# Projections of the mixer branches as three products of rounded high and low parts

## What is computed

```python
def trunk_layer(x, cond, P, l, ctx):
    ...
    ob = chunk_gmlp(bu, bv, P['b_v_norm'][l], P['b_ws'][l], P['b_bs'][l])
    ...
    gates = jax.nn.sigmoid(gl.astype(jnp.float32)).astype(x.dtype).reshape(b, s, N_BRANCH, D_MODEL)
    merged = (gates[:, :, 0] * (oa.reshape(b, s, A_Q) @ P['w_a_o'][l])
              + gates[:, :, 1] * (ob @ P['w_b_o'][l])
              + gates[:, :, 2] * (oc.reshape(b, s, C_Q) @ P['w_c_o'][l]))
    x = x + g1 * (merged @ P['w_out'][l])
    ...
    x = x + g2 * expert_choice_moe(h2, P['w_router'][l], P['b_router'][l], P['w_gate'][l], P['w_up'][l], P['w_down'][l])
    return x, new
```

## Time and profile before

| | us |
|---|---|
| median of 3 runs | 2548.26 (2548.24 to 2552.01) |
| profiled execution | 2548.74 |
| its span, first to last instruction | 2546.9 |
| TensorE busy (matmul) | 2301.7, 90% |
| weight loads | 1765.2, 69% |
| VectorE busy | 1641.2, 64% |
| ScalarE busy | 1205.8, 47% |
| GpSimd busy | 283.7, 11% |

### The profile page before, as it was taken

How to read it: one execution, slowest core, us unless ns; L and a number is a source line. 1 busy time by engine, 2 the same in 40 slices (tenths; PEclk the granted TensorE clock), 3 DMA queues, 4 the chain that set the end, 5 groups by cost and what they waited for, 6 DMA issues and landing times.

```text
span 2546.9 us, 37561 instructions
## 1 busy us (share of the span) xinstructions
PE 2301.7 (90%) x14585; PEld 1765.2 (69%) x14585; DVE 1641.2 (64%) x1927; ACT 1205.8 (47%) x1348; POOL 283.7 (11%) x246
## 2 busy tenths in 40 slices
PE   3998899999769999999959988999995999999997
PEld 1777779899546666666647777898994666666664
DVE  1345545534768889888942465454355888988885
ACT  3223323312257777777732232233122677777773
POOL 1012000001121111110011020000012101111101
PEclk8999999999879999999969999999996999999998
DMA  9351110105589999999944410111154999999995
GB/s 333 133 172 63 53 59 34 59 34 182 206 301 365 374 373 373 373 379 375 366 148 166 168 67 20 59 34 59 53 198 167 337 372 373 373 374 376 378 377 184
DMA packets 271390, 566.10 MB, mean 222 GB/s; under 512 B 10568, under 2 KB 12680, under 8 KB 271216
## 3 DMA queue, kind: packets, MB, share of 16 engines
q1 hardware_dynamic: 254848, 509.64, 55.5%
q0 software_dynamic: 14512, 48.05, 6.4%
q10 hardware_dynamic: 1904, 6.62, 0.7%
HBM read 542.71 MB, written 24.18 MB: 223 GB/s over the span
## 4 chain that ended last, share of the span: by engine, by line
PE 83%; DVE 5%; DMA 4%; issue 4%; ACT 3%; DVEq 0%; POOL 0%; SPq 0%; ACTq 0%; POOLq 0%
PE ps L1069 39%; PE ps L770 26%; PE ps L918 6%; PE ps L852 3%; PE ps L894 2%; DMA ring<-in_w_down 2%; PE ps L877 1%; PE ps L710 1%; PE ps L724 1%; DMA ring<-in_w_mod 1%; PE ps L1059 1%; PE ps L988 1%; DVE w_lo L1794 1%; DMA ring<-in_w_in 1%; ACT w_hi L1378 1%
## 5 line engine op out<-in xcount | busy, mean ns | idle before, releaser
L1794 DVE TENSOR_TENSOR w_lo<-ring,w_hi 128x2048 fp32r<-128x2048 f32 x378 | 864.6, 2288 | 134.9 <-ACT w_hi L1378 134.1
L1378 ACT ACTIVATE w_hi<-ring 128x2048 fp32r<-128x2048 f32 x384 | 736.7, 1920 | 315.8 <-PE ps L1069 257.8
L1069 PE MATMUL ps<-w_hi,xT 128*80 128x512 f32 x2048 | 649.1, 396 | 2.2 <-DVE xT L1800 2.2
L770 PE MATMUL ps<-WH,HTH 128*128 128x256 f32 x1840 | 540.3, 294 | 14.7 <-ACT Y L1304 9.0
L770 PE MATMUL ps<-ringL,HTH 128*128 128x256 f32 x1840 | 520.1, 283 | 0.0
L770 PE MATMUL ps<-WH,HTL 128*128 128x256 f32 x1840 | 519.6, 282 | 0.0
L1069 PEld LDWEIGHTS ps<-w_hi,xT 128*80 128x80 f32 x2048 | 306.0, 149 | 173.1 <-issue 4.6
L1069 PE MATMUL ps<-w_lo,xT 128*80 128x512 f32 x1024 | 406.0, 397 | 0.0
L770 PEld LDWEIGHTS ps<-WH,HTH 128*128 128x128 f32 x1840 | 351.6, 191 | 42.2 <-issue 23.1
L770 PEld LDWEIGHTS ps<-ringL,HTH 128*128 128x128 f32 x1840 | 351.9, 191 | 0.8
L770 PEld LDWEIGHTS ps<-WH,HTL 128*128 128x128 f32 x1840 | 351.0, 191 | 0.0
(11 more groups left out here) (198 smaller groups left out, 2145.0 us busy)
## 6 DMA issues: line engine op xcount, KB each, us to landing
ring<-in_w_gate SPq DMA_DIRECT2D x128, 1024.0 KB, 11.3
ring<-in_w_up SPq DMA_DIRECT2D x128, 1024.0 KB, 10.2
ring<-in_w_down SPq DMA_DIRECT2D x128, 1024.0 KB, 11.8
ring<-in_w_mod SPq DMA_DIRECT2D x23, 2048.0 KB, 8.1
ring<-in_w_in SPq DMA_DIRECT2D x18, 2048.0 KB, 7.9
ring<-in_w_out SPq DMA_DIRECT2D x4, 2048.0 KB, 10.6
ring<-in_w_o SPq DMA_DIRECT2D x4, 1536.0 KB, 6.4
Y<-x_save POOLq DMA_DIRECT2D x10, 512.0 KB, 7.4
```

The costliest lines, as they stand in the source:

```text
L770: last = nc.tensor.matmul(dst, a[:, t, k], w, start=k == 0 and i == 0, stop=k == KB - 1 and i == 2)
L1069: last = nc.tensor.matmul(ps[0:CE, bank], lhs[:, a, kb], w[:, u, k], start=kb == 0 and i == 0, stop=kb == KB - 1 and i == 2)
L1378: nc.scalar.activation(w_hi[:, u % UB], ring[:, raw[0], 4 * (u % 2):4 * (u % 2) + 4], ACT.Copy).then_inc(hi_ready, 1)
L1794: TT(w_lo[:, u % UB], ring[:, raw[0], 4 * (u % 2):4 * (u % 2) + 4], w_hi[:, u % UB].bitcast(f32), ALU.subtract).then_inc(lo_ready, 1)
```

## The change

Both operands of a projection are split into high and low parts and the projection becomes three f32r products for each 128 rows of w_o. New tiles of the type f32r lie over existing ones (`QKr` over `QK`, `Yr` over `Y`, `SCr` over `SC`), in regions that are free at the time.

```diff
+        qoH = QKr[:, 0:8 * 640].rearrange("p (s n) -> p s n", s=8)
+        A_LOW = (2048, 2432, 1536, 3072, 3456)
...
+        def out_low(k, t):
+            if k < 3:
+                return SCr[:, A_LOW[t] + 128 * k:A_LOW[t] + 128 * k + 128]
+            if k == 5:
+                return yr[:, t, CQ + 256:CQ + 384]
+            return yr[:, t, BU + 128 * (k % 3):BU + 128 * (k % 3) + 128]
...
+        def quarter_hi(l, v):
+            n = len(BRANCH[STAGES[v // 4]])
+            if v % 2:
+                a = SCr[:, 768:768 + 256 * n]
+            else:
+                a = ringL[:, SLOT[l]["o", v // 4]].rearrange("p k n -> p (k n)")[:, 3 * D:3 * D + 256 * n]
+            return a.rearrange("p (k n) -> p k n", k=n)
... (GpSimd, ahead of the load of g1)
-                pool.wait_ge(side_done, l * NSIDE + SIDE["kc", NT - 1] + 1)
+                pool.wait_ge(side_done, l * NSIDE + SIDE["proj", 39] + 1)
... (TensorE, project)
-                    if r == 0:
-                        arrived(pe, l, ("o", s))
+                    if t == 0:
+                        pe.wait_ge(wq_lo, l * 12 + 4 * s + q + 1)
...
-                        last = nc.tensor.matmul(ps[:, 7, 0:256], qoT[:, k, 128 * t:128 * t + 128],
-                                                w[:, i, 256 * q:256 * q + 256], start=i == 0, stop=k == ks[-1])
+                        a = qoH[:, k, 128 * t:128 * t + 128]
+                        for n, (x_, w) in enumerate(((a, wh[:, i]), (a, wl[:, i]), (out_low(k, t), wh[:, i]))):
+                            last = nc.tensor.matmul(ps[:, 7, 0:256], x_, w, start=i == 0 and n == 0,
+                                                    stop=k == ks[-1] and n == 2)
... (ScalarE)
                 def mixed_out(t):
...
-                    nc.scalar.activation(qoT[:, 6:8, 128 * t:128 * t + 128],
-                                         ps[:, 7, 0:256].rearrange("p (s n) -> p s n", s=2), ACT.Copy).then_inc(side_free, 1)
+                    nc.scalar.activation(qoH[:, 6:8, 128 * t:128 * t + 128],
+                                         ps[:, 7, 0:256].rearrange("p (s n) -> p s n", s=2), ACT.Copy).then_inc(mix_hi, 1)
+                def split_quarter(v):
+                    if v % 4 == 0:
+                        arrived(act, l, ("o", v // 4))
+                    if v >= 2:
+                        act.wait_ge(side_done, l * NSIDE + SIDE["proj", 5 * v - 6] + 1)
+                    nc.scalar.activation(quarter_hi(l, v), quarter(l, v, ring), ACT.Copy).then_inc(wq_hi, 1)
... (ScalarE and VectorE alike, at the end of extra)
+                    if kind == "gate" and i % 20 == 1:
+                        split_quarter(i // 5)
+                    if kind == "proj" and i % 5 == 0 and i % 20 < 15:
+                        split_quarter(i // 5 + 1)
... (VectorE)
                 def weighed(j):
...
-                    nc.vector.tensor_copy(qoT[:, 3 * br + g, 128 * t:128 * t + 128], ps[:, 5, 0:128]).then_inc(o_evac, 1)
+                    if j == 0:
+                        dve.wait_ge(g_saved, 16 * MOD2 * (l + 1))
+                    if br == 0 and t == 3 and g == 0:
+                        dve.wait_ge(side_done, l * NSIDE + SIDE["kc", NT - 1] + 1)
+                    o = qoH[:, 3 * br + g, 128 * t:128 * t + 128]
+                    nc.vector.tensor_copy(o, ps[:, 5, 0:128]).then_inc(o_hi, 1)
+                    dve.wait_ge(o_hi, l * NP + j + 1)
+                    TT(out_low(3 * br + g, t), ps[:, 5, 0:128], o.bitcast(f32), ALU.subtract).then_inc(o_evac, 1)
+                def mixed_low(t):
+                    dve.wait_ge(mix_hi, l * NT + t + 1)
+                    TT(yr[:, t, BU:BU + 256].rearrange("p (s n) -> p s n", s=2),
+                       ps[:, 7, 0:256].rearrange("p (s n) -> p s n", s=2),
+                       qoH[:, 6:8, 128 * t:128 * t + 128].bitcast(f32), ALU.subtract).then_inc(side_free, 1)
+                def split_quarter(v):
+                    dve.wait_ge(wq_hi, l * 12 + v + 1)
+                    TT(quarter(l, v, ringL), quarter(l, v, ring), quarter_hi(l, v).bitcast(f32), ALU.subtract
+                       ).then_inc(wq_lo, 1)
```

More of the change, by code:

```diff
@@ L243, in build @@
             WH = sa("WH", [128, 2, KB, 256], f32r)
+            with ExitStack() as rounded:
+                Yr = sa("Yr", [128, NT * QKV], f32r, rounded)
             Y = sa("Y", [128, NT * QKV])
+            with ExitStack() as rounded:
+                SCr = sa("SCr", [128, 4096], f32r, rounded)
             SC = sa("SC", [128, 4096])
+            with ExitStack() as rounded:
+                QKr = sa("QKr", [128, 8 * 640 + 2 * 768], f32r, rounded)
             QK = sa("QK", [128, 8 * 640 + 2 * 768])
@@ L276, in build @@
         qoT = QK[:, 0:8 * 640].rearrange("p (s n) -> p s n", s=8)
+        qoH = QKr[:, 0:8 * 640].rearrange("p (s n) -> p s n", s=8)
+        yr = Yr[:, :].rearrange("p (t c) -> p t c", t=NT)
+        A_LOW = (2048, 2432, 1536, 3072, 3456)
         kT = QK[:, 8 * 640:8 * 640 + 2 * 768].rearrange("p (b n) -> p b n", b=2)
@@ L367, in build @@
         o_evac = sem("o_evac")
+        o_hi = sem("o_hi")
+        mix_hi = sem("mix_hi")
+        wq_hi = sem("wq_hi")
+        wq_lo = sem("wq_lo")
         merged_ready = sem("merged_ready")
@@ L1674, in extra @@
                         mlp(i)
+                    elif kind == "mix":
+                        mixed_low(i)
+                    if kind == "gate" and i % 20 == 1:
+                        split_quarter(i // 5)
+                    if kind == "proj" and i % 5 == 0 and i % 20 < 15:
+                        split_quarter(i // 5 + 1)
                 for j in range(NP + 1):
```

5 lines of the change are left out of this document (4 added, 1 removed).

## The result

The changed kernel takes 2559.99 us (median of 5 runs, 2558.64 to 2562.11) against 2548.26 us before; the ratio is 1.0044, with a 95% interval of 1.0032 to 1.0055. It is slower by 11.7 us, where 5.3 us less were forecast. The profiled execution has a span of 2558.2 us, 11.3 more than before.

What follows compares the result with a forecast made beforehand. TensorE's in-order stream was taken to bound the kernel. A gain of 25.2 us, less 16.8 of waits and 3.1 of clock, made 5.3 us off the median of 2548.26: 2543.0 us, range 2539 to 2549.

Steps and rivals of the forecast that it cites:

- tail pair of gate and projection: In the mixer's tail, a gate group and projection together would take 3.88 us, where they took 4.11.
- wait in pair 5: TensorE's mlp(1) would start 3.2 us later per layer, waiting for VectorE's low part behind the rotation of tile 4.
- pairs 6 to 9: In branch b, VectorE's subtraction frees the bank later, 0.40 us four times a layer: 1.6 us.
- the projection's gain: Nine rounded products replace three fp32 ones: 0.236 us less per projection, 0.157 in branch b, 25.2 us in all.
- start of the second stage: Splitting w_o and the output write delay the turned block's copy, so TensorE's second turn: 1.9 us a layer.
- start of the third stage: ScalarE's rounding of w_o after gate 41 delays its turned-block copy, then weigh(29) and projection 40: 1.2 us a layer.
- output write and splits, ends of the branches: Output write about 0.33 us longer, hidden except at two branch ends a layer, 0.25 each: 0.5 us; later splits cost nothing.
- the clock term: Longer waits in pairs 5 to 9 bring two more half-clock spells per layer, 0.77 us each: 3.1 us.
- My rival: Half clock covers the gate groups of pairs 5 to 9 in both layers, 15.3 us: 2555.2 us, slower; chance 0.09.
- The rival of three passes of four: Rounded products take one of fp32's four passes each, so projections gain 34.5 us: 2533.7 us; chance 0.06.
- the rival that VectorE would be late in the even pairs of the second stage: Added output write delays the turned block's copy, 0.34 us in 12 pairs, 4 us: 2547.0 us; chance 0.10.

Runs made afterwards that it cites:

- e9: The changed kernel with unneeded products on TensorE behind every mix, 30 behind the first and 8 behind each of the other four; 2542.10 us.
- e6: As e5, but VectorE does the low part of an output behind the next pair's weights and row maximum; 2532.26 us.
- e5: The changed kernel with branch b's bank freed by one ScalarE copy, plus the w_o quarters split at other places on VectorE and ScalarE; 2536.80 us.
- e3: The kernel before, fp32 products kept, with only the bank's release moved to a VectorE subtraction, placed as in the change; 2576.39 us.
- e1: The changed kernel, with VectorE doing the low part of mix(0) ahead of the rotation of tile 4 in pair 5; 2553.81 us.
- e4: The changed kernel with 30 unneeded products on TensorE between mixed(0) and mlp(1); 2548.33 us.
- e7: As e6, with six unneeded rounded products behind each mix on TensorE; 2528.60 us.
- e8: As e7, with eleven more unneeded products on TensorE in the last two pairs of the second stage; 2523.65 us.

## Why the prediction was wrong

The waits and their places were told rightly, and most of their sizes. At full clock (e9 against before, first layer, with 0.236 us taken off before for each projection of a stretch, 0.157 in branch b):

| term, us a layer | predicted | measured | from |
|---|---|---|---|
| tail pair of gate and projection | 3.88 | 3.89 | 42 to 59 |
| wait in pair 5 | 3.2 | 3.1 | 13.92 - 10.83 |
| pairs 6 to 9 | 1.6 | 1.8 | 4 x (0.30 + 0.16, the projection's gain) |
| start of the second stage | 1.9 | 1.9 | 15.40 - (13.98 - two projections, 0.47) |
| start of the third stage | 1.2 | 1.15 | 6.36 - (5.44 - 0.24) |
| output write and splits, ends of the branches | 0.5 | 1.4 | 0.52 in gate 30 to 31, 0.57 in 35 to 36, 0.35 in 39 to 40 |
| all other stretches | 0 | 0.8 | 0.1 to 0.3 each in 15 to 20, 23 to 30, 31 to 39 and the tail |

Together that is 10.1 us a layer, where 8.4 were predicted, against a gain of 12.6. The rotation ahead of `mixed_low(0)`, the late output write ahead of the rotation, TensorE's wait released by the low part: all as told, and in its place. The output write was under-sized: in after TensorE waits 0.32 us ahead of the first turn of gate 30 to 31, released by VectorE's weights, where before it had no wait; putting the low part later (e6 against e5) gets back 0.32 and 0.12 us and loses 0.18. The price of the third stage's start came out by luck: 511.0 + 0.8 + 0.9 is 512.7 and not 512.9, which makes 0.9 us and not 1.2.

**The step that failed is the clock term**: "I take two more per layer of 0.77: 3.1 us", for both layers together. The runs showed about 19 us in its place. Four things in it were wrong.

First, the unit. 0.77 was pair 8 compared with pair 7. Pair 8 is the shorter of the two at full clock, which the trace of before could not show. Against itself the spell costs 1.51 us (e6).

Second, the kind of spell. The spell that I had seen came behind waits of about 1 us. I wrote down that pair 5's wait would be 3.8 us long, as an argument on chances, and priced it like the short ones. It cost 4.85 us. The next pair had a spell of its own, 1.55 us (13.55 against 12.00 in e9).

Third, where it falls. I looked at pairs 5 to 9 alone. At gate 39 to 40 and 41 to 42 the change has a spell too, 1.5 us each (13.74 against 12.21, 7.90 against 6.36 in e9), and before had none at either.

Fourth, what it covers. My rival took half clock as 1.53 us for a gate group, ten times at most, 2555.2 us. The half clock of pair 5 begins with `mlp(1)` and holds for the turn, the weighing, the scores and the masks, and the gate group only has its first half of it. Half clock costs what TensorE has to do while it lasts, whatever that is: 14.02 against 9.19 us busy.

With the measured sizes the first layer has 4.85 + 1.55 in pairs 5 and 6, 1.5 at gate 39 and 1.54 at gate 41, 9.4 us, and the second about as much. From gate 0 to 59 of both layers that makes -24.3 + 20.2 + 19 = +15 us (two projections a layer stand behind gate 59), against 15.6 in the traces. The spans of the two traces differ by 11.3 only because work outside these stretches was 4.3 us shorter in that of after, which no term of mine foresaw and no run explains. So the rival that I had given 0.09 was the nearest in kind, slower by half clock, and the range had no room for it at its real price: it ended at 2549, and the case above it at 2555.2.

The Trainium skill has the mechanism, "TensorE: Matmul & The Clock Gate", section HAM oscillation: an engine that waits for its operands before each piece of work can start each piece at half clock, so a wait costs more than its length. The traces of after and e9 agree, with 3.1 us of wait and 4.85 of clock for one such wait, and e3 repeats both in the kernel before (18.79 us against 10.83). The section's case is a wait for DMA in every step; here it was one wait of 3.71 us, and smaller ones of about 1 us (e1, second layer) did it in some places and not in others.

The rival of three passes of four fell: a rounded product takes 0.12 us also in the projections, and the tail is at 3.89 us and not at 3.79 (4.11 less a quarter of 1.29). So did the rival that VectorE would be late in the even pairs of the second stage: from gate 24 on their stretches take 7.1 to 7.3 us against 7.43, and TensorE is busy in all of it.

## What to carry to other kernels

When an edit adds or lengthens a wait of TensorE, price it as the wait plus the work behind it at half clock, and look for that price in the busy time of unchanged instructions (84 records, 9.19 to 14.02 us), not in the idle time. Before a second engine is put between a bank and its release, look at what that engine has queued ahead of it; if the first engine can empty the bank in one copy, as here, the second can work from SBUF, and here a low part that stood ready 2.7 us after the rounded one held up nothing in that pair. Where a wait can't be removed, a few products that nobody needs may be worth more than they cost: 30 a layer took 11.7 us off this kernel.

## What the runs showed of the hardware

- TensorE's clock fell to half behind a wait of 3.71 us in all four cases (two layers of after, two of e3), and in none of the four where products filled it (e4, e9), though in one of these the next two stretches had a spell each (17.52 and 17.30 us, e4). In after it fell in the middle of the wait (0.76 in the slice from 277 to 278 us) and was back at 291, 11.6 us after the wait's end.
- Where waits of about 1 us recur, the same records with the same waits ran at 1.00 and at 0.67 in the two layers of one execution (11.28 and 15.44 us, e1). Two traces of the kernel before agreed with each other in every stretch of the mixers, while 23 timed executions of it spread from 2544.18 us at a mean clock of 0.963 to 2555.65 at 0.956. I can't say what sets it.
- With 0.7 us filled behind each `mixed` the spell in pair 8 was gone from all four layers traced (11.78 to 10.26 us, e7 and e8); without it e6 had lost it in one layer of two. With eleven products more gate 39 to 40 was at full clock in both layers (12.42 us, e8); of the sixteen layers in the eight other traces with the change it was in three (12.0 to 12.2 us, against 13.4 to 15.0). That is one trace, so the link is likely and not shown.
- A rounded product of 128x128 weights and 256 columns comes every 0.12 us, three of them 0.36 us, against 0.43 for one fp32 product.
